# Hybrid attention and gating layer on eight cores: each tile's weighted values put directly behind the next tile's scores, and full products allowed into the scores' PSUM banks

## What is computed

```python
h = rmsnorm(x, norm_g)
proj = h @ w_in + b_in                                  # 1024 -> 2816 columns
q, k, v, z_a, u_s, v_s, z_s = split(proj)               # 512,128,128,512,512,512,512
# banded attention: blocks of 128 queries see their own and the previous block's keys,
# 0 <= q - k < 128; 8 query heads of 64, 2 key/value heads, a learned sink per head
p = exp(scores); probs = p / (sum(p) + exp(sink))
attn = (probs @ v) * silu(z_a)
# spatial gating in chunks of 128 positions, a lower-triangular 128x128 W_s per channel group
sgu = gelu(u_s) * (W_s @ layernorm(gelu(v_s)) + b_s) * silu(z_s)
out = rmsnorm(x + concat(attn, sgu) @ w_out + b_out, final_norm_g)
```

## Time and profile before

| what | value |
|---|---|
| time, median of 3 runs | 520.51 us (520.2 to 520.75) |
| time of the profiled execution | 519.93 us |
| its span, slowest core (core 5) | 518.4 us |
| spans of the 8 cores | 514.2 to 518.4 us |
| mean granted TensorE clock of core 5 | 0.978 of full speed |
| PE busy | 490.8 us (95%) |
| ACT / DVE / POOL busy | 335.4 / 298.3 / 235.9 us (65 / 58 / 46%) |
| chain of work that ended last | PE 77%, POOL 7%, ACT 4%, DMA 4%, DVE 3%, issue 3% |

### The profile page before, as it was taken

One profiled execution on the slowest core, in us unless ns is written; L12 is line 12 of the kernel. 1 busy time (PEld: TensorE's weight loads), 2 busy tenths in 40 slices (PEclk: granted clock), 3 DMA queues, 4 the chain that ended last, 5 costly groups with the idle time before them and its releaser, 6 DMA issues.

```text
span 518.4 us, 10260 instructions; the slowest of 8 cores (514.2 to 518.4 us)
## 1 busy us (share of the span) xinstructions
PE 490.8 (95%) x3443; PEld 235.9 (46%) x3443; DVE 298.3 (58%) x432; ACT 335.4 (65%) x555; POOL 235.9 (46%) x272
## 2 busy tenths in 40 slices
PE   6798889899999999999999999999999989999993
PEld 2356345344454445444454445444454434544441
DVE  3865867463647455465646554465556446666575
ACT  4235677566768486766868486774859467757325
POOL 2101788463245515482364614563364774645313
PEclk9599999899999999999999999999999999999997
DMA  8999995910036813490229713292226203231025
GB/s 236 328 337 330 314 256 89 240 48 36 0 123 178 189 50 114 127 257 24 82 83 233 174 43 123 89 259 59 83 82 189 57 2 115 89 123 42 1 83 202
DMA packets 44019, 71.11 MB, mean 137 GB/s; under 512 B 27552, under 2 KB 27552, under 8 KB 43968
## 3 DMA queue, kind: packets, MB, share of 16 engines
q1 hardware_dynamic: 42480, 67.91, 43.6%
q0 software_dynamic: 1200, 2.25, 2.8%
q10 hardware_dynamic: 288, 0.31, 0.2%
HBM read 49.48 MB, written 16.78 MB: 128 GB/s over the span
## 4 chain that ended last, share of the span: by engine, by line
PE 77%; POOL 7%; ACT 4%; DMA 4%; DVE 3%; issue 3%; SPq 0%; POOLq 0%; DVEq 0%; ACTq 0%
PE pp L535 38%; PE pp L828 20%; PE pp L599 6%; PE pp L723 3%; PE pp L560 3%; PE pp L732 2%; DMA xa<-x 2%; POOL xe L780 2%; PE pp L680 1%; PE pp L584 1%; PE pp L645 1%; POOL xa L780 1%; POOL uT L651 1%; DMA xe<-x 1%; DMA out<-xe 1%
## 5 line engine op out<-in xcount | busy, mean ns | idle before, releaser
L535 PE MATMUL pp<-xT,w_fm 128*128 128x512 bf16 x1088 | 246.8, 382 | 4.4 <-ACT xT L526 1.3
L535 PEld LDWEIGHTS pp<-xT,w_fm 128*128 128x128 bf16 x1088 | 104.6, 98 | 132.7 <-issue 10.0
L828 PE MATMUL pp<-w_out_bf,mixT 128*128 128x512 bf16 x512 | 119.1, 381 | 2.1 <-issue 2.1
L828 PEld LDWEIGHTS pp<-w_out_bf,mixT 128*128 128x128 bf16 x512 | 47.9, 98 | 61.4 <-issue 7.0
L780 POOL TENSOR_TENSOR xe<-xe,bout_sb 128x1024 f32<-128x1024 f32 x28 | 65.8, 2353 | 21.3 <-DVE xe L845 10.1
L758 POOL TENSOR_TENSOR mixT<-LR,zaT 128x512 bf16<-128x512 f32 x28 | 32.4, 1156 | 69.7 <-DVE LR L754 68.7
L742 ACT ACTIVATE LR<-pp,esink 128x128 f32<-128x128 f32 x128 | 36.5, 368 | 33.6 <-PE pp L732 23.4
L599 PE MATMUL pp<-w_vs,xT 128*128 128x512 bf16 x224 | 50.0, 379 | 2.2 <-DVE Cmat L880 1.7
L833 DVE TENSOR_TENSOR xe<-pp,xe 128x512 f32<-128x512 f32 x56 | 38.5, 688 | 22.3 <-PE pp L828 21.5
L845 DVE SCALAR_TENSOR_TENSOR xe<-xe,st_fr,gf_sb 128x1024 f32<-128x1024 f32 x28 | 35.9, 1283 | 25.0 <-POOL st_fr L843 9.5
L707 ACT ACTIVATE PT<-pp 128x1536 bf16<-128x1536 f32 x31 | 44.5, 1436 | 6.5 <-PE pp L687 6.5
(11 more groups left out here) (91 smaller groups left out, 585.1 us busy)
## 6 DMA issues: line engine op xcount, KB each, us to landing
xa<-x SPq DMA_DIRECT2D x32, 512.0 KB, 6.0
xe<-x SPq DMA_DIRECT2D x28, 512.0 KB, 4.2
out<-xe SPq DMA_DIRECT2D x28, 512.0 KB, 2.8
xe<-w_in SPq DMA_DIRECT2D x12, 512.0 KB, 12.6
mixT<-w_in SPq DMA_DIRECT2D x10, 512.0 KB, 15.1
w_out_bf<-w_out POOLq DMA_DIRECT2D x8, 256.0 KB, 14.4
out<-xa SPq DMA_DIRECT2D x3, 512.0 KB, 2.8
LR<-sgu_wT SPq DMA_DIRECT2D x1, 512.0 KB, 17.2
```

The source lines that it names most:

```text
L535: ins = e.matmul(bank(h), lhsT=w_fm[:, FM.index(cb), k, :], rhs=xT[:, xb, k, :], start=(k == 0), stop=(k == 7))
L828: ins = e.matmul(bank(h), lhsT=mixT[:, mb, ec, tt * 128:(tt + 1) * 128], rhs=w_out[:, ec, hf * 512:(hf + 1) * 512], start=(ec == 0), stop= ...
```

## The change

Three things are changed. The scores of every tile but the first of a phase are placed by the scheduler only once the previous tile's mask is estimated done, and they also take that previous tile's two value banks; the values of the previous tile then have no other condition left than the scores in front of them, so they follow directly. The number of banks in class `P` is no longer capped (they still come from 4 to 7). And from the moment the last scores of a phase are placed until the silu phase, full products may also take banks 0 to 3.

```diff
+            if o.mode == "quad":
+                t = max([t] + [d.fin + LAT for d in o.after])
             o.nready = t
...
+        scores_left = {}
+        for o in ops:
+            if o.mode == "quad":
+                scores_left[o.gate] = scores_left.get(o.gate, 0) + 1
+
         def pick_banks(o):
 
             t, got, taken = 0.0, [], set()
             for b in o.alloc:
-                if used[b.cls] + b.size + sum(x.size for x, _ in got if x.cls == b.cls) > self.CAPS[b.cls]:
+                if b.cls != "P" and used[b.cls] + b.size + sum(x.size for x, _ in got if x.cls == b.cls) > self.CAPS[b.cls]:
                     return None
                 best = None
-                for pref, i in enumerate(self.PLACES[b.cls]):
+                places = self.PLACES[b.cls]
+                if b.cls == "P" and scores_left.get(cp, 0) == 0 and cp % 3 != PH_SILU and cp > 1:
+                    places = self.PLACES["P"] + self.PLACES["G"]
+                for pref, i in enumerate(places):
...
+            if o.mode == "quad":
+                scores_left[o.gate] -= 1
...
+        for tiles in chain.values():
+            for (_, mask, values), (scores, _, _) in zip(tiles, tiles[1:]):
+                scores.after += (mask,)
+                values.after += (scores,)
+                V = values.alloc[0]
+                scores.alloc += (V,)
+                V.users.insert(0, scores)
+                values.alloc, values.uses = (), (V,)
```

More of the change, by code:

```diff
@@ L659, in mix_part @@
                      writes=[("mixS", mb, jj), ("mst", 2 * mb), ("mst", 2 * mb + 1)], prio=v0, port=True)
+        chain = {}
         def attention(st, j):
@@ L689, in mms @@
                 return ins
-            G.op("pe", mms, reads=[("qT", qb, c) for c in range(4)] + [("kT", (n - 1) // 4 % 3), ("kT", n // 4 % 3)], cost=0.45, alloc=[S],
+            o = G.op("pe", mms, reads=[("qT", qb, c) for c in range(4)] + [("kT", (n - 1) // 4 % 3), ("kT", n // 4 % 3)], cost=0.45, alloc=[S],
                  prio=v0 - 10, mode="quad", gate=ph)
+            chain.setdefault(ph, []).append([o])
             if first:
@@ L711, in attention @@
             G.op("act", ex, uses=[S], writes=[("PT", p2)], cost=2.0 if first else 1.47, prio=v0 - 0.5, phase=ph)
-            G.op("dve", mk, reads=["msk"], writes=[("PT", p2)], cost=0.96, prio=v0 - 0.5, port=True)
+            o = G.op("dve", mk, reads=["msk"], writes=[("PT", p2)], cost=0.96, prio=v0 - 0.5, port=True)
             V = Bank("V", 2)
@@ L735, in attention @@
             vkeys = [("v", 0, s1), ("v", 64, s2), ("v", 64, s1)] + ([] if first else [("v", 0, s0)])
-            G.op("pe", mmpv, reads=[("PT", p2)] + vkeys + ["ones64"],
+            chain[ph][-1].append(o)
+            o = G.op("pe", mmpv, reads=[("PT", p2)] + vkeys + ["ones64"],
                  cost=0.80, alloc=[V], prio=v0 - 11, mode="col")
+            chain[ph][-1].append(o)
             lb = n % 2
```

## The result

The changed kernel took 524.44 us in its profiled execution and 523.10 in another, against a median of 520.36 (519.42 to 520.75) before: ratio 1.0063, 95% interval 1.0035 to 1.0091, so 3.3 us slower. Two more executions of it, 543.45 and 578.27, are left out, since the cores of one die had a lower granted clock in each (0.94 and 0.87). In a later set of runs the ratio was 1.0066 (1.0040 to 1.0091). The forecast was 517.4 with a range up to 521.3, and a chance of 0.13 for slower: wrong in sign.

The account below looks back on a forecast made before the run. PE was taken as the bound, busy 95% of the span; -2.1 - 2.6 + 1.1 + 0.5 = -3.1 against 519.93 gave 516.8, plus 0.6 for the median 517.4; own range 515.5 to 519.3, overall 513.5 to 521.3.

Parts of the forecast that it names:

- The mixing: Three stages lose the output product before the mixing; normalised tiles about 2 earlier, cost nothing, or 1.0 in three places.
- Term 4: Stages: scores wait for `LR` two tiles back, a tie at 4.9 in ten short stretches; 0.5 lost, bounds 0 and 1.0.
- the output banks don't hinder: Within the stages' term: evacuating output banks needs 0.7 per 1.73, so no cost was booked.
- Term 1: Start of the attention, first stage: old loss 4.2, new waits 2.1, so 2.1 gained; bounds nothing and 4.2.
- The first new wait: First stage: third tile's scores wait 1.7 for the first tile's `LR` on DVE.
- Term 2: Last attention: three old waits of 1.09, 1.01 and 0.47 vanish, 2.6 gained; bounds 0 and 2.6.
- the first mask: Last attention: first mask ends 14.1 after the mixing, and PE wants it at 15.9.
- Term 3: Joints of scores then values on PE save 0.09 to 0.10 each, the old order 0.21; 1.1 lost.
- The one on the other side: Rival, chance 0.10: scores' new bank condition is the bound, every short stretch pays, at 0.7 each the time is 523.9.
- The waits only move: Rival, chance 0.15: the start gains nothing, half of the last attention's gain returns; 520.3.

Follow-up runs that it names:

- roots_clear: Changed kernel with the bias add among POOL's root pairs scheduled behind the last `vln` in the three middle stages that waited; ratio to before 1.0012.
- late_g: Changed kernel with the planner told longer durations for POOL's two small root operations, which also linked them with DVE's operations; ratio to before 0.9989.
- own_banks: Changed kernel with the values taking their own two banks again, scores and values still linked in the schedule; ratio to before 1.0021.
- first_only: Changed kernel with the chain of scores and values in the first stage alone; ratio to before 0.9983, 518.73 us.
- first_adds: Kernel with the chain in the first stage alone, two of that stage's POOL bias adds moved behind the second and third tiles' masks; ratio to before 1.0001.
- last_adds: Changed kernel with two of POOL's four bias adds in the last attention moved behind its first mask; ratio to before 1.0050.
- cover_gone: Kernel before the change, with the output product between gating products and mixing moved behind the mixing in five middle stages; ratio to before 0.9993.

## Why the prediction was wrong, step by step

**The mixing, costed at nothing, is the step that gave the change most of its loss.** The prediction said that the moved bias add brings the normalised tiles "about 2 earlier", and that a failed cover would be 1.0 in three places. From the gating products' start to the last `vln`'s end it was 289.36 - 274.40 = 14.96 before and 291.87 - 277.50 = 14.37 after: 0.6 earlier, not 2, while the due time moved by a product, 1.73. I had followed the add and not the gate product that came in front of the last `vln` with a link. Measured cost 1.9 (0.6, 0.6 and 0.7), where the fallback that I named was 1.0 in each of the three places; roots_clear takes the waits of two places away, late_g and own_banks all three.

**Term 4**, 0.5 for the new condition: the waits for `LR` cost 0.24 in the second stage and 0.3 in the last attention, none in the other short stretches, so its size held. But "the output banks don't hinder" failed. DVE in order of time, fourth stage:

```profile
250.87 0.95 DVE L725 TENSOR_TENSOR PT<-PT,msk 128x1536 bf16<-128x1536 bf16 x1
251.74 0.69 DVE L850 TENSOR_TENSOR xe<-pp,xe 128x512 f32<-128x512 f32 x1
```

Scores and values claim banks 0 to 5 together, so full products alternate between 6 and 7, and an evacuation behind a mask makes the product behind it late. PE in order of time there:

```profile
250.60 1.89 PE L547 MATMUL pp<-xT,w_fm 128*128 128x512 bf16 x8
252.57 1.89 PE L845 MATMUL pp<-w_out_bf,mixT 128*128 128x512 bf16 x8
```

The first takes 1.97 instead of 1.74. That is the likeliest reading of some 0.2 each in two places of the fourth and the sixth stage, 0.9 in all; no run tested it alone.

**Term 1**, 2.1 gained: measured 1.0 by the ledger's medians, 0.9 by first_only. The first new wait was sized well (1.7 forecast, 1.1 to 1.5 measured). The second was forecast at 0.3 to 0.4 and is 1.5. On DVE the `LR` stands behind `xn`, which waits for a root of four columns on POOL, and behind an evacuation of `vs_f`, and these end 1 us later than I put them. Of that 0.8 is the root: I gave the pair 1.4, and it took 2.2, since a mask ran beside it. DVE and then POOL in order of time in the changed kernel (core 2), then POOL in first_adds (core 4), where no mask does:

```profile
91.64 0.96 DVE L725 TENSOR_TENSOR PT<-PT,msk 128x1536 bf16<-128x1536 bf16 x1 [0.95 <-POOL st_ms L490]
```

```profile
91.67 1.84 POOL L493 TENSOR_TENSOR st_rs<-st_ms,neghalf 128x4 f32<-128x4 f32 x1
```

```profile
89.30 1.04 POOL L493 TENSOR_TENSOR st_rs<-st_ms,neghalf 128x4 f32<-128x4 f32 x1
```

All eight cores of either run agree. first_adds also shows that the row of operations on DVE sets the end: with the short root, the fourth tile's scores wait as long.

**Term 2**, 2.6 gained: nothing. On a quiet core (core 4) the waits before were 0.56, 1.01 and 0.47, so 2.04; the 2.57 that the prediction booked from the earlier trace rows was a slower core's. After they are 0.41, 0.61, 0.28 and 0.20, so 1.5. Of the 0.5 gained, the joints of this stretch take back 0.4: five that saved 0.21 against seven that save 0.09. The step that failed is the first mask, forecast to end 14.1 behind the mixing: it ended at 427.29, 17.06 behind 410.23. POOL has three bias adds before it, at 410.89, 420.60 and 423.88; one of 2.35 and its hand-overs is what the forecast's 14.1 had no room for. last_adds puts back 0.6 in that stretch.

**Term 3**, joints: right. The pair is 1.44 long with its entry, and the rule of the Trainium skill, "TensorEngine Tiling (Array Packing)", section "Key Properties", that a change of tiling mode drains TensorE, points the way the rows went: the joint in the new order saves 0.09 and not 0.21. The stages that differ from before by their joints alone lose 0.60 against 0.61 and 0.61 against 0.55, so in a stage the term is within 0.1.

**The sum.** Forecast 3.1 faster, and by the ledger 2.3 slower: 5.4 apart. Term 2 is the largest part (2.1 of waits that stayed), then the mixing (1.9), term 1 (1.1) and the output banks (0.9, argued), while the joints cost some 0.4 less than forecast. Had the mixing alone been right, the forecast would still have been 3.5 too good.

**The rivals.** The one on the other side had the right sign by the wrong mechanism: it made scores wait in every short stretch, and they waited in two places. "The waits only move" describes the last attention and half the start.

## What to carry to other kernels

Where a list scheduler rebuilds the whole order, the loss comes in where a transfer of cover happened that nobody asked for: list every long operation that lost its neighbour, and follow each queue that feeds it to the last linked operation, not to the one that was seen to move. A wait read on the slowest core may hold that core's own clock or transfers; take it from a quiet core before it is booked as a gain. Undo the parts of a change one by one over the stages of the program: here a chain in one stage out of eight kept the gain and none of the loss.

## What the runs showed that I had not expected

- The fall of the clock after the idle 2.09 does not always come. In cover_gone, with the same order there, the output product behind such an idle took 1.85 on cores 2 and 6 (no fall; the granted clock of core 2 was 1.00 in it) and 2.80 on core 0 (0.63). In the kernel before it fell on six cores, whose start loses 5.0 to 6.6, and not on cores 1 and 6, which lose 3.5. The start of the chained kernels loses 3.8 to 4.6, and up to 5.1 on die 1 of the chip with the lower clock there.
- Two operations that the planner doesn't link can still slow each other. The root of four columns on POOL took 1.02 in the stages and 1.83 in the first one of the changed kernel, where DVE's mask ran beside it for 0.93; in the kernel before it was 1.04 on six cores and 1.56 on the two where a mask ran beside it for 0.66.
- A duration in a planner can be a switch. Two small operations were told to be longer by 0.15 and 0.05, the second crossed the bound of 0.6 from which operations are linked, and the time moved by 4.0 us on one chip.
